# Two of four heads of a recurrent solve written to the other half of the PSUM partitions, with other orders of work in the attentions, a LayerNorm and the first mixer

## The chip, the cores and the metric

The kernel runs on one core of one Trainium2 chip, in one launch. The metric is the time of an execution in device microseconds (us). TensorE (PE) multiplies, VectorE (DVE), ScalarE (ACT) and GpSimd (POOL) do the elementwise work, and SyncE (SP) starts the weight transfers. The engines run their own instruction streams in order and wait for one another through semaphores.

## What is computed

The reference is a chain of small transformer-like blocks over 512 tokens of width 1024, all in float32. Cut to what the change touches:

```python
def _mixer_hgrn2_conv(h, ...):              # "l0"
    proj = h @ w_in                         # q, f, i, g and two halves of a gated unit
    f = lb + (1.0 - lb) * sigmoid(fz)       # the gates; then log(f), its running sum, 1 - f
    o = _hgrn2_chunkwise(silu(qz), f, iz)
    c = _causal_depthwise_conv(glu_a * sigmoid(glu_b), dw_w, dw_b)   # 31 taps
# attentions: xa0 and xa1 (4 heads), moba (8), diff (4 x 2), fox (8), each softmax(q k + bias) v
def _rwkv7_scan(r, w, k, v, kk, a):         # 8 heads of 64
    def step(state, inp):
        sa = einsum('bhij,bhj->bhi', state, -kk_t)
        state = state * w_t + sa * (kk_t * a_t) + v_t * k_t
        return state, einsum('bhij,bhj->bhi', state, r_t)
h = _layer_norm(DEEPNORM_ALPHA * h + ffn, ln2_g, ln2_b)              # "end2"
```

The scan over 512 tokens is done in chunks of 64. In a chunk the tokens' mutual dependence is a triangular system, whose inverse is built by products of 64x64 matrices (squares, fourth and eighth powers of the part inside 16-token blocks, then the part between blocks) and applied to the right sides.

## The kernel before

**Weights.** All weights come from memory as 527 units of 128x1024 floats. SP brings a unit to RW (4 buffers), ACT rounds it to WH (`w_hi`, line 269), POOL subtracts, WL = RW - WH (line 3289), and PE multiplies with it in three passes for each of eight blocks (lines 274 to 276: hi x hi, hi x lo, lo x hi). WH and WL have 3 buffers each (SPLIT = 3), so ACT may round unit u once PE has done unit u - 3. Where in ACT's stream a unit is rounded is written out by hand: each stage calls `w_hi(act, st, v)`, "all units up to v".

**Order.** The program is a list of stages (`PLAN`), `Linear`, `Pairs`, `LayerNorm`, `PairAttention` and free `Stage`s, each of which says what PE, ACT and DVE do in it. An engine walks the list in order. A `st.do(..., name)` marks an instruction, and `st.wait(name)` waits for one.

**l0** (0 to 193 us). Linears for the gated unit, q, f, i and g, with the 31 taps of the convolution spread over DVE and POOL between their outputs; POOL does one tap behind each of a run of units (line 3289 and after). Behind f stand the gates: `h_gates` on DVE (lines 1460 and 1462), then `h_ln`, the logarithm on ACT (line 1468).

**Attention.** `PairAttention` runs over iterations `it`, TT = 4 query blocks for each group of heads, with two streams s. PE: `scores(it)`, then `turn(it - 2)`, which transposes the probabilities of two iterations before; with each fourth turn the `outputs` of a group. ACT: `exps(it)` (line 1212), then the copies `pt` of turned blocks (line 1202). DVE: maxima (1225), `normalize` (1237 to 1247) and `take` (1254). `values` marks an attention whose value products are made in the middle of it.

**LayerNorm.** PE sums (mean, line 1013), ACT squares (1036), PE sums the squares (1003), ACT takes the root (1038), and both write the normalised tensor. Only the norm end2 has `late`, the norm of the next block, that follows at once. The sums into SD that PE waits for are DVE adds (line 691).

**The solve** (1874 to 1996.5 us). The 8 heads are two groups g of four, and there are four blocks t of 128 tokens, two chunks each; a pass is one (t, g), with 9 solve steps (`solve_pe`, `solve_act`, `solve_dve`) and 6 steps of the state. A matrix tensor of a group (D, DT, K, O, F, E) is 128x256: chunk 0 of the four heads in partitions 0 to 63, chunk 1 in 64 to 127, a head in 64 columns. The list `ORDER` lets the second group run 7 steps behind the first (LAG = 7, STEPS = 15), so steps of two passes alternate on every engine. The products of a group go through `quarters` (matmuls on line 2249), which reads a 64x64 block of one partition half and writes the same half of PSUM:

```python
for n in heads:
    for r in halves:
        last = mm(out[r, n * w:(n + 1) * w], L[r, n * 64:(n + 1) * 64], R[r, n, :], start=True, stop=True)
```

Step 1 makes D squared (d2) and its transpose (d2t); step 2 d4, d4t and F2 = F + E F; step 3 d8 and F4; step 4 F8; step 5 the coupling of blocks m, mt, and b0 = F RHS; steps 6 and 7 the corrections b1 and b2. Between them ACT copies the powers from PSUM and DVE adds each F and each right side. Group g uses the PSUM banks from B = 4 g.

## Time and profile before

| | us |
|---|---|
| median of 3 runs | 3428.56 |
| lowest, highest | 3426.52, 3431.85 |
| profiled execution | 3425.99 |
| its span, first to last instruction | 3423.9 |
| PE busy in it | 3297.7 (96%) |
| DVE, ACT, POOL busy | 1337.0, 1204.4, 1329.8 |
| mean granted clock of PE, share of full | 0.989 |

Busy time is the union of an engine's instructions, POOL's included. Idle time of PE is where a released wait can pay. A wait in a list is put down to the instruction that came last before it ended. A timeline row gives the start, the length and the count of like instructions in a row; a group's length runs from its first start to its last end, and a matmul record carries a tail of some 0.22 to 0.28 us beyond the spacing at which such matmuls start. In the windows, PEclk is the granted clock of PE as a share of 2.4 GHz; 0.5 is its lower level, 1.2 GHz.

### The profile page before, as it was taken

How to read it: one execution, taken by the hardware profiler on the slowest of the kernel's cores; microseconds unless marked ns; L12 is line 12 of the kernel's file. 1: busy time of each engine (PE TensorE's matmuls, PEld its weight loads, DVE VectorE, ACT ScalarE, POOL GpSimd, SP SyncE). 2: the span in 40 equal slices, each digit the busy share in tenths (PEclk: the TensorE clock that was granted, in tenths of full speed). 3: DMA queues.
4: the chain of work that ended last, by engine and by line, in shares of the span. 5: the costliest groups of instructions: out<-in, count | busy, mean ns of one | idle time of the engine just before them, and what ended most of it. 6: DMA issues, size and time to landing. Idle time of an engine off the chain costs nothing. (4 is left out here: it accounts for less than half of the span.)

```text
span 3423.9 us, 41030 instructions
## 1 busy us (share of the span) xinstructions
PE 3297.7 (96%) x17376; PEld 2650.1 (77%) x17376; DVE 1337.0 (39%) x1994; ACT 1204.4 (35%) x1817; POOL 1329.8 (39%) x555
## 2 busy tenths in 40 slices
PE   8889999999999999999999999999899999999998
PEld 6678788887778788886677976888688778778886
DVE  8963431214343421213448652001373261134733
ACT  4443432224343422224444333222334432242332
POOL 4743244444254244443143023444344324414442
PEclk9999999999999999999999999999999999999999
DMA  4232132222232122323123032222232212202231
GB/s 154 84 100 87 54 99 98 93 99 92 68 100 98 56 92 99 99 95 104 55 82 125 8 112 75 98 99 97 76 111 93 74 56 99 90 34 99 93 122 68
DMA packets 83005, 302.48 MB, mean 88 GB/s; under 512 B 9060, under 2 KB 10888, under 8 KB 81928
## 3 DMA queue, kind: packets, MB, share of 16 engines
q1 hardware_dynamic: 78368, 280.55, 24.7%
q10 hardware_dynamic: 4456, 19.33, 1.5%
q8 instruction: 137, 2.24, 0.3%
q14 instruction: 44, 0.36, 0.0%
HBM read 290.39 MB, written 9.44 MB: 88 GB/s over the span
## 5 line engine op out<-in xcount | busy, mean ns | idle before, releaser
L3289 POOL TENSOR_TENSOR WL<-RW,WH 128x1024 fp32r<-128x1024 f32 x527 | 1294.1, 2459 | 2067.2 <-ACT WH L269 2066.7
L274 PE MATMUL PS<-XH,WH 128*128 128x512 f32 x2968 | 1169.5, 394 | 46.4 <-DVE XL L932 16.2
L275 PE MATMUL PS<-XL,WH 128*128 128x512 f32 x2968 | 1159.9, 391 | 0.0
L276 PE MATMUL PS<-XH,WL 128*128 128x512 f32 x2968 | 1159.4, 391 | 0.0
L269 ACT ACTIVATE WH<-RW 128x1024 fp32r<-128x1024 f32 x527 | 553.6, 1053 | 799.4 <-PE PS L276 694.3
L274 PEld LDWEIGHTS PS<-XH,WH 128*128 128x128 f32 x2968 | 560.2, 189 | 185.7 <-POOL WL L3289 30.0
L276 PEld LDWEIGHTS PS<-XH,WL 128*128 128x128 f32 x2968 | 560.0, 189 | 117.9
L275 PEld LDWEIGHTS PS<-XL,WH 128*128 128x128 f32 x2968 | 560.4, 189 | 116.3 <-issue 2.2
L274 PE MATMUL PS<-YH,WH 128*128 128x512 f32 (+1 forms) x928 | 350.4, 378 | 8.0 <-POOL WL L3289 6.6
L275 PE MATMUL PS<-YL,WH 128*128 128x512 f32 (+1 forms) x928 | 349.2, 376 | 0.0
L276 PE MATMUL PS<-YH,WL 128*128 128x512 f32 (+1 forms) x928 | 349.1, 376 | 0.0
L501 DVE TENSOR_TENSOR SG<-PS,NR 128x512 f32<-128x512 f32 x136 | 93.5, 691 | 534.3 <-PE PS L276 533.9
L274 PEld LDWEIGHTS PS<-YH,WH 128*128 128x128 f32 x928 | 176.5, 190 | 42.2 <-POOL WL L3289 7.4
L276 PEld LDWEIGHTS PS<-YH,WL 128*128 128x128 f32 x928 | 176.6, 190 | 31.4
L275 PEld LDWEIGHTS PS<-YL,WH 128*128 128x128 f32 x928 | 176.5, 190 | 31.0
L487 ACT ACTIVATE SG<-SG 128x512 f32<-128x512 f32 x80 | 50.6, 632 | 367.7 <-DVE SG L501 367.6
L640 DVE TENSOR_TENSOR YL<-A,YH 128x512 fp32r<-128x512 f32 x66 | 50.3, 773 | 262.6 <-ACT YH L636 262.6
L408 DVE TENSOR_TENSOR A<-PS,NR 128x512 f32<-128x512 f32 (+1 forms) x84 | 53.3, 638 | 164.6 <-PE PS L276 164.2
L636 ACT ACTIVATE YH<-A 128x512 fp32r<-128x512 f32 x66 | 40.7, 629 | 211.3 <-PE PS L276 211.3
L523 DVE TENSOR_TENSOR A<-SG,PS 128x512 f32<-128x512 f32 x30 | 20.6, 688 | 213.9 <-PE PS L276 202.6
L1225 DVE TENSOR_REDUCE SM<-PS 128x1 f32<-128x256 f32 (+3 forms) x128 | 55.6, 470 | 105.2 <-PE PS L3054 55.0
L429 DVE TENSOR_TENSOR X<-X,PS 128x512 f32<-128x512 f32 x40 | 27.5, 687 | 140.4 <-PE PS L276 140.4
(525 smaller groups left out, 3190.3 us busy)
## 6 DMA issues: line engine op xcount, KB each, us to landing
RW<-in_units SPq DMA_DIRECT2D x527, 512.0 KB, 3.3
spill<-X ACTq DMA_DIRECT2D x2, 2048.0 KB, 7.6
X<-in_xT SPq DMA_DIRECT2D x8, 256.0 KB, 5.8
A<-spill ACTq DMA_DIRECT2D x1, 2048.0 KB, 8.9
X<-spill ACTq DMA_DIRECT2D x4, 512.0 KB, 6.0
X<-spill ACTq DMA_DIRECT2D x1, 2048.0 KB, 7.9
out_T<-X ACTq DMA_DIRECT2D x4, 512.0 KB, 3.0
spill<-X ACTq DMA_DIRECT2D x1, 1536.0 KB, 5.1
```

Source lines behind the costliest of these rows:

```text
L269: nc.scalar.activation(WH[:, u % SPLIT, :], RW[:, u % RAW, :], ACT.Copy).then_inc(split_hi, 1)
L274: mm(out, hi, xh, start=first, stop=False)
L275: mm(out, hi, xl, start=False, stop=False)
L276: return mm(out, lo, xh, start=False, stop=last)
L408: ins = nc.vector.tensor_tensor(self.dst(j), bank(e % 4, self.cols), self.late.r, ALU.mult)
L429: ins = nc.vector.tensor_tensor(x, x, b, ALU.add)
L487: st.do(nc.scalar.activation(SG[:, j, :], SG[:, j, :], self.func), f"pair{e}")
L501: st.do(nc.vector.tensor_tensor(dst, bank((e + q) % 4), self.late.r, ALU.mult), name)
L636: st.do(nc.scalar.activation(YH[:, self.hslot(k), :], T(k), ACT.Copy), f"{self.name}.hi{k}")
L640: st.do(nc.vector.tensor_tensor(YL[:, self.hslot(k), :], T(k), YH[:, self.hslot(k), :].bitcast(F32), ALU.subtract), f"{self.name}.lo{k}")
L1225: st.do(nc.vector.tensor_reduce(SM[:, c:c + 1], bank(2 * (it % 2) + s, self.blocks_of(it) * P), AX.X, ALU.max, negate=True), f"{self.id}.m ...
L3289: nc.gpsimd.tensor_tensor(WL[:, u % SPLIT, :], RW[:, u % RAW, :], WH[:, u % SPLIT, :].bitcast(F32), ALU.subtract).then_inc(split_done, 1)
```

## The change

**Solve.** A new function `crossed` makes ten of a pass's products. Heads 0 and 1 write as before, heads 2 and 3 write to the other partition half, in the next bank, and the four (two heads, two halves) stand next to each other in PE's stream. With two such levels a head is back in its half. So that each operand is in the half where the next product reads it, the operands change: F2 = (I + D2) F is now a product alone, with I + D2 made by a DVE add of the identity (p1), the same for p2, p3, pm and pk, and ACT or DVE only copies the results out. F8 and b2 still go through `quarters`. ACT takes half of the copies of the right sides.

**Attention.** In every fourth iteration ACT does the pt copies ahead of the exps. Where there are `values`, the scores of iterations 2 and 3 both stand ahead of the first turn. With `lam` (diff alone) the outputs of a group stand behind the turn of one iteration later, and DVE's take follows.

**LayerNorm end2.** The two unit roundings ahead of the squares now stand one behind the squares and one behind the root.

**l0.** `eager` and `ahead` round each unit one unit earlier in the gated unit, q, f and g. The gates move from DVE to ACT, ahead of the logarithm. POOL's taps begin one unit earlier.

```diff
-                                w_hi(act, st, u + SPLIT)
+                                w_hi(act, st, u + SPLIT + (j in self.ahead))
...
+                            w_hi(act, st, u + SPLIT + self.eager)
...
-                if self.rms is not None or self.late is not None:
+                if self.rms is not None:
                     w_hi(act, st, st.unit + SPLIT - 2)
...
+                if self.late is not None:
+                    w_hi(act, st, st.unit)
...
+                if self.late is not None:
+                    w_hi(act, st, st.unit)
...
-                    if (0 if not self.values else 2) <= it < self.n:
+                    if it == 2 and self.values:
+                        self.scores(st, 2)
+                        self.scores(st, 3)
+                    elif it < self.n and not (it < 4 and self.values):
                         self.scores(st, it)
...
+                    if self.lam is not None and it % TT == 3 and it > TT:
+                        self.outputs(st, it // TT - 1)
                 self.outputs(st, self.groups - 1)
 
             def turn(self, st, it):
-                if it % TT == 0 and it:
+                if self.lam is None and it % TT == 0 and it:
                     self.outputs(st, it // TT - 1)
...
-                    if self.led <= it < self.n:
+                    sooner = it < self.n and it % TT == TT - 1
+                    if self.led <= it < self.n and not sooner:
                         self.exps(st, it)
...
+                    if sooner:
+                        self.exps(st, it)
...
-                    if it % TT == 2 and it >= TT:
+                    if it % TT == (2 if self.lam is None else 3) and it >= TT:
...
+        glu = Pairs("l0.glu", 4, at(0), ACT.Sigmoid, of=1, ready="n0", late=n0, between=glu_dve, between_act=glu_act, eager=1)
...
-        def h_gates(st):
-            st.settle()
+        Linear("l0.f", dst=at(12), func=ACT.Sigmoid, late=n0, between=lambda st, j: conv(st, 5 if j < 3 else 0), between_act=f_act, ahead=range(4))
+
+        vs(lambda st: conv(st, 3))
+
+        def h_ln(act, st, e):
             for h in range(4):
-                st.do(v.tensor_scalar(T(12 + h), T(12 + h), SM[:, LB + 4 + h:LB + 5 + h], SM[:, LB + h:LB + h + 1], ALU.mult, ALU.add))
-            st.settle()
-            st.do(v.tensor_scalar(W2(32, 4), W2(12, 4), -1.0, 1.0, ALU.mult, ALU.add), "h.f")
-            conv(st, 3)
-        vs(h_gates)
-
-        def h_ln(act, st, e):
-            st.wait_ge(*reached("h.f"))
+                st.do(a_.activation(T(12 + h), T(12 + h), ACT.Identity, bias=SM[:, LB + h:LB + h + 1], scale=SM[:, LB + 4 + h:LB + 5 + h]))
+            st.settle()
+            st.do(a_.activation(W2(32, 4), W2(12, 4), ACT.Identity, bias=cst("one"), scale=-1.0), "h.f")
+            st.settle()
             st.do(a_.activation(W2(12, 4), W2(12, 4), ACT.Ln), "h.ln")
...
+        def crossed(b, at, L, R, w=64):
+
+            for n in (0, 2, 1, 3):
+                for r in range(2):
+                    o = halves[r if n < 2 else 1 - r]
+                    last = mm(PS[o, b + n // 2, at + n % 2 * w:at + (n % 2 + 1) * w], L[halves[r], n * 64:(n + 1) * 64], R[halves[r], n, :],
+                              start=True, stop=True)
+            return last
+
...
-                st.wait(i + ".d2t_", i + ".f1")
-                st.do(quarters(bank(B), D, by_head(E)), i + ".d4")
-                st.do(quarters(bank(B + 1), E, by_head(D)), i + ".d4t")
-                st.wait(i + ".rhs")
-                st.do(quarters(bank(B + 2), E, by_head(F), heads=LOW), i + ".f2.0")
-                st.do(quarters(bank(B + 3), E, by_head(F), heads=HIGH), i + ".f2.1")
+                st.wait(i + ".d2t_")
+                st.do(crossed(B, 0, D, by_head(E)), i + ".d4")
+                st.do(crossed(B, 128, E, by_head(D)), i + ".d4t")
+                st.wait(i + ".rhs", i + ".f1", i + ".p1")
+                st.do(crossed(B + 2, 0, K, by_head(F)), i + ".f2")
             elif step == 3:
                 st.wait(i + ".d4t_")
-                st.do(quarters(bank(B), DT, by_head(K)), i + ".d8")
-                st.wait(i + ".F2.0")
-                st.do(quarters(bank(B + 2), K, by_head(F), heads=LOW), i + ".f4.0")
-                st.wait(i + ".F2.1")
-                st.do(quarters(bank(B + 3), K, by_head(F), heads=HIGH), i + ".f4.1")
+                st.do(crossed(B, 0, DT, by_head(D)), i + ".d8")
+                st.wait(i + ".F2", i + ".p2")
+                st.do(crossed(B + 2, 0, E, by_head(F)), i + ".f4")
             elif step == 4:
-                st.wait(i + ".d8_", i + ".F4.0")
-                st.do(quarters(bank(B + 2), E, by_head(F), heads=LOW), i + ".f8.0")
-                st.wait(i + ".F4.1")
-                st.do(quarters(bank(B + 3), E, by_head(F), heads=HIGH), i + ".f8.1")
+                st.wait(i + ".p3", i + ".F4")
+                st.do(quarters(bank(B), K, by_head(F)), i + ".f8")
             elif step == 5:
-                st.wait(i + ".F8.0")
-                quarters(bank(B), F, by_head(O), heads=LOW)
-                st.wait(i + ".F8.1")
-                st.do(quarters(bank(B), F, by_head(O), heads=HIGH), i + ".m")
-                st.do(quarters(bank(B + 2), O, by_head(F)), i + ".mt")
-                st.do(quarters(bank(B + 3), F, RHS[g], P, LOW), i + ".b0.0")
-                st.do(quarters(bank(B + 1), F, RHS[g], P, HIGH), i + ".b0.1")
+                st.wait(i + ".F8")
+                st.do(crossed(B + 2, 0, F, by_head(O)), i + ".m")
+                st.do(crossed(B + 2, 128, O, by_head(F)), i + ".mt")
+                st.do(crossed(B, 0, F, RHS[g], P), i + ".b0")
             elif step == 6:
                 st.wait(i + ".mt_")
-                st.do(quarters(bank(B), D, by_head(DT)), i + ".m2t")
-                st.wait(i + ".q0.0")
-                st.do(quarters(bank(B + 2), DT, RHS[g], P, LOW), i + ".b1.0")
-                st.wait(i + ".q0.1")
-                st.do(quarters(bank(B + 3), DT, RHS[g], P, HIGH), i + ".b1.1")
+                st.do(crossed(B + 2, 0, D, by_head(DT)), i + ".m2t")
+                st.wait(i + ".pm", i + ".q0.0", i + ".q0.1")
+                st.do(crossed(B, 0, E, RHS[g], P), i + ".b1")
             elif step == 7:
-                st.wait(i + ".m2t_", i + ".q1.0")
-                st.do(quarters(bank(B + 1), K, RHS[g], P, LOW), i + ".b2.0")
+                st.wait(i + ".pk", i + ".q1.0")
+                st.do(quarters(bank(B), K, RHS[g], P, LOW), i + ".b2.0")
                 st.wait(i + ".q1.1")
-                st.do(quarters(bank(B), K, RHS[g], P, HIGH), i + ".b2.1")
+                st.do(quarters(bank(B + 1), K, RHS[g], P, HIGH), i + ".b2.1")
...
+                st.wait(i + ".d4t")
+                st.do(a_.activation(pair(D), PS[:, B:B + 2, 0:P], ACT.Copy), i + ".d4_")
+                st.wait(i + ".f1")
+                st.do(a_.activation(pair(DT), PS[:, B:B + 2, P:2 * P], ACT.Copy), i + ".d4t_")
+                st.wait(i + ".f2")
+                st.do(a_.activation(pair(F), PS[:, B + 2:B + 4, 0:P], ACT.Copy), i + ".F2")
             elif step == 3:
-                st.wait(i + ".d8")
-                st.do(a_.activation(E, half(B), ACT.Copy), i + ".d8_")
+                st.wait(i + ".f4")
+                st.do(a_.activation(pair(F), PS[:, B + 2:B + 4, 0:P], ACT.Copy), i + ".F4")
+            elif step == 4:
+                st.wait(i + ".f8")
+                st.do(a_.activation(F, half(B), ACT.Copy), i + ".F8")
             elif step == 5:
-                st.wait(i + ".m")
-                st.do(a_.activation(D, half(B), ACT.Copy))
                 st.wait(i + ".mt")
-                st.do(a_.activation(DT, half(B + 2), ACT.Copy), i + ".mt_")
+                st.do(a_.activation(pair(D), PS[:, B + 2:B + 4, 0:P], ACT.Copy))
+                st.do(a_.activation(pair(DT), PS[:, B + 2:B + 4, P:2 * P], ACT.Copy), i + ".mt_")
+                st.wait(i + ".b0")
+                st.do(a_.activation(RHS[g][:, 2:4, :], by_head(bank(B + 1))[:, 0:2, :], ACT.Copy), i + ".q0.1")
...
-            elif step in (2, 3, 4):
-                name = "248"[step - 2]
-                for h in range(2):
-                    two = slice(128 * h, 128 * h + 128)
-                    st.wait(f"{i}.f{name}.{h}")
-                    if h == 0:
-                        st.settle()
-                    st.do(v.tensor_tensor(F[:, two], F[:, two], bank(B + 2 + h)[:, two], ALU.add), f"{i}.F{name}.{h}")
+                st.wait(i + ".d2_", i + ".w")
+                st.do(v.tensor_tensor(wqc(K), wqc(E), mask("eye"), ALU.add), i + ".p1")
+            elif step == 2:
+                st.wait(i + ".d4_")
+                st.settle()
+                st.do(v.tensor_tensor(wqc(E), wqc(D), mask("eye"), ALU.add), i + ".p2")
+            elif step == 3:
+                st.wait(i + ".d8")
+                st.do(v.tensor_tensor(wqc(K), two_banks(B), mask("eye"), ALU.add), i + ".p3")
             elif step == 5:
...
+                st.wait(i + ".b0")
+                st.do(v.tensor_copy(RHS[g][:, 0:2, :], by_head(bank(B))[:, 0:2, :]), i + ".q0.0")
+                st.wait(i + ".mt_")
+                st.do(v.tensor_tensor(wqc(E), wqc(DT), mask("eye"), ALU.add), i + ".pm")
+            elif step == 6:
+                st.wait(i + ".m2t")
+                st.do(v.tensor_tensor(wqc(K), two_banks(B + 2), mask("eye"), ALU.add), i + ".pk")
+                st.wait(i + ".b1")
+                st.do(v.tensor_copy(RHS[g][:, 0:2, :], by_head(bank(B))[:, 0:2, :]), i + ".q1.0")
+            elif step == 7:
+                st.wait(i + ".b2.0")
+                st.do(v.tensor_copy(RHS[g][:, 0:2, :], by_head(bank(B))[:, 0:2, :]), i + ".q2.0")
...
-                if U0["l0.q"] + 3 <= u < U0["l0.q"] + 3 + POOL_TAPS:
-                    pool_tap(pool, u - U0["l0.q"] - 2)
+                if U0["l0.q"] + 2 <= u < U0["l0.q"] + 2 + POOL_TAPS:
+                    pool_tap(pool, u - U0["l0.q"] - 1)
```

Where the solve's products stand on PE, in the first pass, steps 4 to 6 (SG is where group 0's tensors lie; `scalar_steps` and `vector_steps` are the semaphores of ACT and DVE). Before:

```order
L2249 MATMUL PS<-SG 64x64 [waits vector_steps,scalar_steps]
L2249 MATMUL PS<-SG 64x64 x3
L2249 MATMUL PS<-SG 64x64 [waits vector_steps]
L2249 MATMUL PS<-SG 64x64 x3
L2249 MATMUL PS<-SG 64x64 [waits vector_steps]
L2249 MATMUL PS<-SG 64x64 x3
L2249 MATMUL PS<-SG 64x64 [waits vector_steps]
L2249 MATMUL PS<-SG 64x64 x11
L2249 MATMUL PS<-SG 64x128 x8
L2249 MATMUL PS<-SG 64x64 [waits scalar_steps]
L2249 MATMUL PS<-SG 64x64 x7
```

and after the change (line 2267 is the matmul of `crossed`, 2259 that of `quarters`):

```order
L2259 MATMUL PS<-SG 64x64 [waits scalar_steps,vector_steps]
L2259 MATMUL PS<-SG 64x64 x7
L2267 MATMUL PS<-SG 64x64 [waits scalar_steps]
L2267 MATMUL PS<-SG 64x64 x15
L2267 MATMUL PS<-SG 64x128 x8
L2267 MATMUL PS<-SG 64x64 [waits scalar_steps]
L2267 MATMUL PS<-SG 64x64 x7
```

The four half products of F8 with a wait each became one call behind one wait, m and mt follow behind one wait, and b0 is one call of eight.

ACT around the gates of l0 (269 rounds a unit, 373 is the sigmoid, 1468 the logarithm). Before:

```order
L269 ACTIVATE WH<-RW 128x1024 [waits unit_done,raw_full1]
L373 ACTIVATE A<-A 128x512 [waits vector_steps]
L269 ACTIVATE WH<-RW 128x1024 [waits unit_done,raw_full2]
L373 ACTIVATE A<-A 128x512 [waits vector_steps]
L1419 ACTIVATE A<-PS,VEC 128x512
L1468 ACT_TABLE_LOAD [waits vector_steps]
L1468 ACTIVATE A<-A 128x2048 [waits scalar_steps]
L269 ACTIVATE WH<-RW 128x1024 [waits raw_full3,unit_done,scalar_steps]
L269 ACTIVATE WH<-RW 128x1024 [waits unit_done,raw_full0]
```

and after (1474 and 1476 are the gates, 1478 the logarithm):

```order
L269 ACTIVATE WH<-RW 128x1024 [waits unit_done,raw_full2]
L373 ACTIVATE A<-A 128x512 [waits vector_steps]
L269 ACTIVATE WH<-RW 128x1024 [waits unit_done,raw_full3]
L373 ACTIVATE A<-A 128x512 [waits vector_steps]
L1432 ACTIVATE A<-PS,VEC 128x512
L1474 ACTIVATE A<-A,SM 128x512 [waits scalar_steps]
L1474 ACTIVATE A<-A,SM 128x512 x3
L1476 ACTIVATE A<-A,CST 128x2048 [waits scalar_steps]
L1478 ACT_TABLE_LOAD
L1478 ACTIVATE A<-A 128x2048 [waits scalar_steps]
L269 ACTIVATE WH<-RW 128x1024 [waits raw_full0,unit_done,scalar_steps]
L269 ACTIVATE WH<-RW 128x1024 [waits unit_done,raw_full1]
```

One more rounding stands ahead of the last sigmoid, and the gates stand ahead of the logarithm and of the next rounding.

ACT in moba, iterations 6 to 8 (1212 are exps, 1202 the pt copies). Before:

```order
L1212 ACTIVATE A,SM<-PS,SM 128x384 [waits vector_steps] x2
L1202 ACTIVATE A<-PS 128x128 [waits tensor_steps]
L1202 ACTIVATE SG<-PS 128x128 [waits tensor_steps]
L1212 ACTIVATE A,SM<-PS,SM 128x512 [waits vector_steps] x2
L1202 ACTIVATE A<-PS 128x2x128 [waits tensor_steps]
L1202 ACTIVATE SG<-PS 128x2x128 [waits tensor_steps]
L1212 ACTIVATE A,SM<-PS,SM 128x128 [waits vector_steps] x2
```

and after (1225 and 1213):

```order
L1225 ACTIVATE A,SM<-PS,SM 128x384 [waits vector_steps] x2
L1213 ACTIVATE A<-PS 128x128 [waits tensor_steps]
L1213 ACTIVATE SG<-PS 128x128 [waits tensor_steps]
L1213 ACTIVATE A<-PS 128x2x128 [waits tensor_steps]
L1213 ACTIVATE SG<-PS 128x2x128 [waits tensor_steps]
L1225 ACTIVATE A,SM<-PS,SM 128x512 [waits vector_steps] x2
L1225 ACTIVATE A,SM<-PS,SM 128x128 [waits vector_steps] x2
```

The two copies of 128x2x128 passed the exps of 128x512, the fourth of a group.

## Rows read from the trace of the kernel before

**Rows 1.** The page's first section: busy us, share of the span, instructions of each engine.

```profile
PE 3297.7 (96%) x17376; PEld 2650.1 (77%) x17376; DVE 1337.0 (39%) x1994; ACT 1204.4 (35%) x1817; POOL 1329.8 (39%) x555
```

**Rows 2.** The waits of PE, whole span: us in all, times, longest us.

```profile
PE PS L274 <- POOL WL L3289: 16.4, 9, 5.5
...
PE PS L1170 <- ACT A L1202: 14.9, 12, 2.1
```

**Rows 3.** Windows: length, busy of PE, PEld, DVE, ACT, POOL, PEclk, DMA share, GB/s.

```profile
0.00:193.00 193.00, 164.83 (x776) 135.84 (x776) 163.16 (x206) 81.21 (x103) 117.67 (x62) 0.97 0.36 124
...
915.00:980.00 65.00, 55.34 (x329) 38.57 (x328) 31.26 (x85) 35.90 (x106) 7.16 (x4) 0.89 0.08 25
...
1874.00:1996.50 122.50, 120.30 (x3173) 107.32 (x3172) 74.39 (x210) 42.38 (x115) 4.88 (x2) 1.00 0.10 32
...
2984.00:3056.00 72.00, 64.26 (x319) 47.89 (x318) 32.16 (x84) 33.56 (x98) 4.77 (x2) 1.00 0.04 15
```

**Rows 4.** The timeline of PE in the solve: start us, us, what, out<-in, xcount, [idle before].

```profile
1902.87 0.28 PE L2273 MATMUL PS<-A 64*64 64x64 f32 x3
...
1903.70 0.61 PE L2286 MATMUL PS<-A 64*64 64x128 f32 x13
...
1905.38 1.15 PE L2249 MATMUL PS<-SG 64*64 64x64 f32 x32
...
1915.47 0.93 PE L2249 MATMUL PS<-SG 64*64 64x128 f32 x14
1916.18 0.27 PE L2273 MATMUL PS<-A 64*64 64x64 f32 x3
```

**Rows 5.** The timeline of ACT and of DVE in the solve, step 1.

```profile
1906.11 0.38 ACT L2354 ACTIVATE SG<-PS 128x256 f32<-128x256 f32 x1 [0.40 <-PE PS L2249]
...
1908.44 0.52 DVE L2415 TENSOR_TENSOR SG<-SG,PS 128x128 f32<-128x128 f32 x2 [0.75 <-PE PS L2249]
```

**Rows 6.** Waits of PE in l0, 0 to 193 us, then the timeline there.

```profile
PE PS L274 <- POOL WL L3289: 15.1, 8, 5.5
...
117.69 3.79 DVE L1460 TENSOR_SCALAR A<-A,SM 128x512 f32<-128x512 f32 x4 [0.80 <-ACT A L373]
...
124.11 1.91 ACT L1468 ACTIVATE A<-A 128x2048 f32<-128x2048 f32 x1
...
126.05 2.95 ACT L269 ACTIVATE WH<-RW 128x1024 fp32r<-128x1024 f32 x3
...
129.59 0.79 PE L274 MATMUL PS<-XH,WH 128*128 128x512 f32 x1 [5.35 <-POOL WL L3289]
...
168.42 0.58 PE L274 MATMUL PS<-YH,WH 128*128 128x256 f32 x1 [5.52 <-POOL WL L3289]
```

**Rows 7.** The timeline of ACT and PE in moba, iterations 7 and 8.

```profile
941.49 0.38 ACT L1202 ACTIVATE A<-PS 128x256 f32<-128x256 f32 x1
...
942.02 0.85 PE L1170 MATMUL PS<-CST,A 128*128 128x128 f32 x6 [1.27 <-ACT A L1202]
```

**Rows 8.** Waits of PE in moba, 915 to 980 us.

```profile
PE PS L1170 <- ACT A L1202: 6.2, 4, 2.1
```

**Rows 9.** Waits of PE in fox, 2984 to 3056 us.

```profile
PE PS L1170 <- ACT A L1202: 6.0, 4, 2.1
```

**Rows 10.** The timeline of PE in diff.

```profile
1654.99 0.70 PE L1909 MATMUL PS<-A 64*128 64x256 f32 x4 [0.68 <-ACT A L1212]
```

**Rows 11.** The timeline of DVE, POOL and PE in end2.

```profile
2453.57 0.69 DVE L691 TENSOR_TENSOR SD<-SD,X 128x512 f32<-128x512 f32 x1
...
2456.08 5.09 POOL L3289 TENSOR_TENSOR WL<-RW,WH 128x1024 fp32r<-128x1024 f32 x2 [7.79 <-ACT WH L269]
2456.29 5.43 DVE L691 TENSOR_TENSOR SD<-SD,X 128x512 f32<-128x512 f32 x2
...
2461.87 2.04 PE L1013 MATMUL PS<-SD,CST 128*128 128x512 f32 x2 [6.34 <-DVE SD L691]
```

**Rows 12.** Windows, columns as in rows 3: behind end2's wait.

```profile
2460.40:2470.60 10.20, 7.22 (x18) 1.95 (x18) 6.20 (x9) 5.84 (x9) 0.77 (x1) 0.50 0.21 77
```

More of the change, by code:

```diff
@@ L1431, in glu_dve @@
             conv(st, 4)
-        glu = Pairs("l0.glu", 4, at(0), ACT.Sigmoid, of=1, ready="n0", late=n0, between=glu_dve, between_act=glu_act)
+        glu = Pairs("l0.glu", 4, at(0), ACT.Sigmoid, of=1, ready="n0", late=n0, between=glu_dve, between_act=glu_act, eager=1)
         def q_act(st, j):
@@ L1449, in q_dve @@
                 conv(st, 6)
-        Linear("l0.q", dst=at(8), func=ACT.Silu, late=n0, between=q_dve, between_act=q_act, between_pe=q_pe)
+        Linear("l0.q", dst=at(8), func=ACT.Silu, late=n0, between=q_dve, between_act=q_act, between_pe=q_pe, ahead=range(4))
         def f_act(st, j):
@@ L1516, in g_dve @@
             conv(st, (5, 3, 2, 4)[j])
-        Linear("l0.g", dst=at(20), func=ACT.Silu, late=n0, between=g_dve, between_act=g_act)
+        Linear("l0.g", dst=at(20), func=ACT.Silu, late=n0, between=g_dve, between_act=g_act, ahead=range(4))
         Stage(tensor=lambda pe, st, e: st.wait_ge(*reached("mem.lo7")))
@@ L2353, in solve_act @@
                 st.wait(i + ".d2")
-                st.do(a_.activation(E, half(B), ACT.Copy))
+                st.do(a_.activation(E, half(B), ACT.Copy), i + ".d2_")
                 st.wait(i + ".d2t")
```

34 lines of the change are left out of this document (12 added, 22 removed).

## The prediction

> **What bounds the kernel now.** I read the page's first section, then the waits of PE, then the windows, then the timelines of five stages. PE is busy for 3297.7 of 3423.9 us [rows 1], so the matmuls set the time, and an edit pays only where PE stands idle or where its own work shrinks. The list of PE's waits gives the places: 16.4 us for POOL's WL (one of them 5.5) and 14.9 us in 12 waits for the copies of line 1202 in the attentions [rows 2]. The windows say how dense PE is: 164.83 of 193 us busy in l0, 55.34 of 65 in moba at a clock of 0.89, but 120.30 of 122.5 in the solve [rows 3]. So in the solve only fewer matmul slots can help; elsewhere waits can.
>
> **The solve: matmul slots.** `quarters` issues a 64-column product of four heads as 8 matmuls, which are 16 records (two per fp32 matmul). Two calls, 32 records, take 1.15 us with the last one's own 0.22, so 0.93 for both, 0.466 a call [rows 4]. The 128-column calls: 14 records in 0.93, less 0.27, is 7 starts of a pair 0.11 apart, so 8 pairs or 0.87 for 16 records; two records start together, one from each diagonal quarter. Line 2286 already uses all four quarters: 13 records in 0.61, less 0.28, is four records every 0.11 [rows 4]. `crossed` puts heads 2 and 3 into the other output half and the next bank, so I take four at a time: 0.233 a call of 64 columns, 0.436 for 128. A pass (t, g) has eight 64-column calls of this kind (d4, d4t, f2, d8, f4, m, mt, m2t) and two of 128 (b0, b1): 8 x 0.233 + 2 x 0.436 = 2.74 us less. Over 8 passes that is 21.9 us, the upper bound. d2, d2t, f8 and b2 stay.
>
> Not all of it arrives. The first starts of line 2273 in two passes, 1902.87 and 1916.18, are 13.31 us apart [rows 4]. In a pass, steps of the two groups of heads alternate, so that one group's ACT and DVE work hides behind the other's matmuls. These covers shrink, and each level still needs a copy: the copy of d2 starts at 1906.11, 0.29 us after that call's last matmul, takes 0.38 and lands 0.06 later (0.73 to 0.76), and DVE needs 0.52 for two adds of 128x128 [rows 5]. I laid the new steps out one after the other with the old durations of what stays: PE then waits 0.06 for p1, 0.22 for d4t's copy, 0.05 for F2, 0.29 for the state copy, 0.27 for F8, 0.10 for mt's copy, 0.32 for pm, 0.31 for pk and q1, and 0.24 in rests of a few hundredths, 1.86 in all. The engine is in order, so behind each of these stands the partner's next step, which waits too. A pass takes 13.31 - 2.74 + 1.86 = 12.43, **7 us less in 8 passes**. The identity adds (p1, p2, p3, pm, pk) take the place of the six F adds and of b1's and b2's adds on DVE, and ACT takes half of the q copies; neither is half busy. Ends: 3 us (each of the eight waits 0.06 longer) to 12 (a third of them covered).
>
> The rows show two row halves writing one bank (line 2249) and four quarters writing two banks with each row half in its own (line 2286), not both at once, which is what `crossed` does. The Trainium skill, TensorEngine Tiling (Array Packing), section Restrictions and Gotchas, speaks against it: different row tiles cannot access the same PSUM bank at the same time. By that rule `crossed` would save nothing. The pairs of line 2249 at 0.11 are this very case and run at the pace of line 2286's fours [rows 4], so the trace disagrees.
>
> **l0: the weight splits.** PE's listed waits for WL in 0 to 193 us are eight, 15.1 in all [rows 6]; counted as matmul starts later than the usual 0.227 us they are ten and 16.5, and I go by these. The two large ones: ACT's WH comes at 126.05 because it stands behind Ln (124.11 to 126.02), which stands behind the gates on DVE (117.69 to 121.48, and 1.23 more for the 2048 columns), and PE starts 5.35 late at 129.59; the same again at 168.42 with 5.52 [rows 6]. The change makes each WH one unit earlier, so the unit of 129.59 is split before the last sigmoid of f and its wait goes, as do five small ones in front of it (0.24 + 0.51 + 0.17 + 1.15 + 0.39 = 2.5). What is late next: the following WH, which now stands behind gates on ACT. Four of 128x512 at some 0.67, one of 128x2048 at 1.91 (Ln's size [rows 6]), the table load 1.28 and Ln 1.91 are 7.8 us from about 118.5, so WH ends near 127.4 and WL (2.4) near 129.0 to 129.8, where PE, 2.5 us ahead of its old time, is free at 126.6: 2.4 us. By the same walk 1.4 remains before the scan's units and 4.8 of the 5.52. 16.5 - 8.6 = 7.9, **8 us less**. Ends: 6 (the gates 1 us longer, and again at the second place) and 9.5 (with the clock, below). The pool taps, a unit earlier, stand where POOL waited for WH, at nothing; were POOL late there, each costs what the unit's WL slips.
>
> **The attentions.** In every fourth iteration ACT's exps (two of 0.69 plus reads) stand ahead of the pt copies, and PE's next turn waits for these: in moba the copy at 941.49, PE at 942.02 after 1.27 idle [rows 7]. Copies first lets that turn start 1.1 us earlier, but exps end 0.7 later and the next scores wait for them, so 0.5 is left, twice. Moba's four waits of this kind are 6.2 in all [rows 8], the first and the last near 2; these have no such successor, and the scores moved ahead help the first: 2.0 + 1.0 + 1.2 = **4.2** (2.5 to 6). Fox has four too, 6.0 in all [rows 9]; by the same working 0.8 + 2 x 0.6 + 1.3 = **3.3** (2 to 4.5). Diff: 0.68 at 1654.99 [rows 10], twice, and a little at its ends, of which the outputs moved behind the turn cover some: **1.6** (0.5 to 2.5). The two cross-attentions: 0, between -0.6 and +0.6, as their copies gain what their exps lose.
>
> **end2.** Two WH at 2454.95 feed two WL (2456.08, 5.09 us for both), beside which two sum adds on DVE take 5.43 together where one alone takes 0.69; PE waits 6.34 for them [rows 11]. With the WH behind the squares and the root: 5.43 - 1.38 = 4.05, and something of the half clock after the wait (0.50 for 10.2 us [rows 12]), 0.5 to 1. Back comes up to 1 where WL meets line 932, which also reads two tensors of SBUF. **4.5 less** (3 to 5.5). What hides the moved splits: PE does not need them before 2477. The Trainium skill, GPSIMD Engine Reference, section Key points, says that GpSimd shares its SBUF interfaces with VectorE and contends with instructions of two SBUF inputs; by that rule the steps of 2464 to 2476 that read PSUM lose nothing, and the trace agrees for the adds of line 691, which read two and are the slow ones [rows 11].
>
> **Sum.** 7 + 8 + 4.2 + 3.3 + 1.6 + 4.5 = 28.6. The profiled execution took 3425.99 (span 3423.9), so 3397.4; the median of the runs lies 2.57 above it: **3400**. All terms at their good ends give 12 + 9.5 + 6 + 4.5 + 2.5 + 5.5 + 0.6 = 40.6, or 3388; at their poor ends 3 + 6 + 2.5 + 2 + 0.5 + 3 - 0.6 = 16.4, or 3412.
>
> **Rivals.**
> *A, PE stays the bound in the solve.* For it: the stage has hardly a wait now [rows 3]. Against: turnarounds of 0.75 us [rows 5] beside covers of 0.23 to 0.47. It gives 15 more: 3385.
> *B, the waits come back in the in-order ACT queue.* The later exps, gates and copies make half of the gains of l0 and the attentions vanish (8.5), and the solve gives 4: 3400 + 8.5 + 3 = 3411. For it: a wait of 1.27 is worth 0.5 in my own working. Against: the first and last turns, and end2, have nothing behind.
> *C, crossing quarters do not overlap.* Then `crossed` costs what `quarters` did, the solve gains nothing and pays 1.86 x 8 = 15 of waits where its new chains are longer: 3400 + 7 + 15 = 3422. Against: rows 4, as above.
> *D, slower: the clock.* After end2's wait the granted clock was 0.50 (1.2 GHz, half of 2.4) for 10.2 us [rows 12], and in moba, where PE was busy 85% and no wait of rows 8 passes 2.1, its mean was 0.89 [rows 3]. The solve's PE share falls from 98% to 85%. At half clock its 8 x 10.57 = 85 us of matmuls need 85 more, with the 15 of waits covered: +70, 3470. It decides against the change from 41% of the stage (28.6 / 70). Against: fox, with waits as long and PE busy 89%, kept 1.00 [rows 3, 9].
>
> **Chances.** Forecast 0.58, A 0.13, B 0.19, C 0.05, D 0.05. The range 3388 to 3412 takes in the forecast with its bounds and B. A measurement of this kernel tells some 0.2% (7 us) from no change: faster is forecast, A and B, 0.90; within it C, 0.05; slower D, 0.05.
>
> **What would show it.** In the solve, groups of four records per 0.057 us in `crossed` and passes 12.4 us apart (A: 10.6; C: 13.3 or more; D: clock 0.5). In l0, no wait at the unit after f and a wait of 2 to 3 us one unit later. In moba and fox, the turn's wait under 0.3 and a new one of scores for ACT exps. In end2, the sum adds at 0.69 and PE's wait near 2.3. I am wrong if the solve's turnarounds are longer or better covered than laid out, or if the gates on ACT take well over 4.6 us.

## The result, and the profile after

The changed kernel takes 3394.6 us (median of 4 runs, 3392.35 to 3397.95) against 3430.2 us for the kernel before in the same comparison: a ratio of 0.9898, with a 95% interval of 0.9881 to 0.9915, so 29 to 41 us less. The ratio and its interval are worked out from all runs of both kernels, so they need not be the quotient of two medians, here or below. The forecast was 3400, its range 3388 to 3412, and it had 28.6 us less. The profiled execution took 3397.95 (span 3396.1), 27.8 us less in the span than the profiled one before.

In the lines below an engine's idle time ahead of an instruction stands in square brackets, with what ended it. The page of the kernel after, first section, answers to [rows 1]:

```profile
PE 3285.8 (97%) x17376; PEld 2633.8 (78%) x17376; DVE 1320.4 (39%) x1957; ACT 1218.5 (36%) x1854; POOL 1330.2 (39%) x555
```

PE is busy 11.9 us less, the rest of the 27.8 is idle time that went. The waits of PE over the whole span, in all, times, longest, answer to [rows 2]:

```profile
PE PS L274 <- POOL WL L3311: 4.9, 4, 2.2
...
PE PS L1014 <- DVE SD L692: 2.3, 1, 2.3
PE PS L1818 <- ACT A L1225: 2.3, 3, 1.5
...
PE PS L3071 <- ACT X L1225: 2.2, 3, 1.5
...
PE PS L1180 <- ACT A L1213: 1.4, 4, 0.3
```

The 16.4 us for POOL's WL are 4.9. The 14.9 us in 12 waits for the pt copies are 1.4 in 4; new in their place are waits of scores for exps (lines 1818 and 3071), 2.3 and 2.2 us. The windows, with the columns of rows 3, are of l0, moba, diff, the solve and fox:

```profile
0.00:182.00 182.00, 162.14 (x776) 135.06 (x776) 154.36 (x201) 86.88 (x107) 118.54 (x62) 0.99 0.38 131
...
904.00:965.00 61.00, 54.98 (x366) 39.32 (x365) 35.56 (x88) 38.27 (x110) 11.68 (x6) 1.00 0.11 35
1613.00:1669.00 56.00, 51.62 (x240) 33.89 (x239) 32.87 (x77) 28.16 (x83) 4.88 (x2) 0.91 0.06 21
1857.90:1973.30 115.40, 108.74 (x3173) 90.96 (x3172) 70.03 (x177) 51.40 (x147) 4.86 (x2) 1.00 0.11 34
...
2958.00:3028.00 70.00, 65.53 (x321) 48.33 (x321) 33.09 (x87) 34.88 (x105) 5.43 (x3) 1.00 0.05 16
```

The same weight multiplications stand in the same order in both traces, so the start of one and the same matmul can be compared ahead of a stage and behind it. That gives what each stage gained, in us, for two traces of the changed kernel (the second is experiment e7), beside the forecast:

| stage | forecast | first trace | second trace |
|---|---|---|---|
| l0 | 8 | 11.2 | 11.2 |
| moba | 4.2 | 8.5 | 7.8 |
| diff | 1.6 | -1.7 | 0.1 |
| solve | 7 | 7.1 | 6.2 |
| end2 | 4.5 | 3.6 | 4.6 |
| fox | 3.3 | 2.7 | 2.6 |
| everything else | 0 | -4.3 | -2.0 |
| sum to the last weight multiplication | 28.6 | 27.1 | 30.5 |

**The solve.** The timeline of PE in the solve answers to [rows 4]:

```profile
1885.76 0.27 PE L2294 MATMUL PS<-A 64*64 64x64 f32 x2
...
1888.36 1.15 PE L2259 MATMUL PS<-SG 64*64 64x64 f32 x32
...
1890.00 1.13 PE L2267 MATMUL PS<-SG 64*64 64x64 f32 x48
...
1891.48 0.73 PE L2267 MATMUL PS<-SG 64*64 64x64 f32 x32
...
1897.96 0.27 PE L2294 MATMUL PS<-A 64*64 64x64 f32 x2
```

Line 2267 is `crossed`. The 48 records of d4, d4t and f2 take 1.13 us, less the last one's 0.22 and a gap of 0.19 between two starts ahead of f2, which waits for p1: 0.72, or 0.24 a call, where a `quarters` call is still 0.466 (32 records of line 2259 in 1.15). d8 and f4 are 32 records in 0.73 less 0.22, 0.255 a call. The marks of two passes, 1885.76 and 1897.96, are 12.20 apart; the seven marks of the stage give 15.25, 12.54, 12.20, 12.35, 12.38, 12.35 and 12.29, where the trace before has 15.23, 13.40, four times 13.31, and 13.44.

**l0.** The timeline of ACT, then of POOL, around the gates answers to [rows 6]:

```profile
110.81 1.06 ACT L269 ACTIVATE WH<-RW 128x1024 fp32r<-128x1024 f32 x1 [1.06 <-PE PS L276]
113.64 0.63 ACT L373 ACTIVATE A<-A 128x512 f32<-128x512 f32 x1 [1.77 <-DVE A L408]
...
114.88 2.94 ACT L1474 ACTIVATE A<-A,SM 128x512 f32<-128x512 f32 x4
117.85 2.01 ACT L1476 ACTIVATE A<-A,CST 128x2048 f32<-128x2048 f32 x1
...
121.18 1.92 ACT L1478 ACTIVATE A<-A 128x2048 f32<-128x2048 f32 x1
123.12 2.01 ACT L269 ACTIVATE WH<-RW 128x1024 fp32r<-128x1024 f32 x2
...
112.39 2.41 POOL L3311 TENSOR_TENSOR WL<-RW,WH 128x1024 fp32r<-128x1024 f32 x1
...
124.26 2.40 POOL L3311 TENSOR_TENSOR WL<-RW,WH 128x1024 fp32r<-128x1024 f32 x1 [6.57 <-ACT WH L269]
```

The unit that came 5.35 us late is rounded at 110.81, ahead of the last sigmoid of f at 113.64. The next unit's WL ends at 126.66, and PE starts it without a wait: in 60 to 137 us the list of PE's waits is empty.

**end2.** The timeline answers to [rows 11]:

```profile
2433.84 1.42 DVE L692 TENSOR_TENSOR SD<-SD,X 128x512 f32<-128x512 f32 x2
...
2435.40 2.04 PE L1014 MATMUL PS<-SD,CST 128*128 128x512 f32 x2 [2.32 <-DVE SD L692]
...
2444.11 2.34 POOL L3311 TENSOR_TENSOR WL<-RW,WH 128x1024 fp32r<-128x1024 f32 x1 [18.27 <-ACT WH L269]
...
2447.13 2.06 DVE L1087 SCALAR_TENSOR_TENSOR X<-A,VEC,PS 128x512 f32<-128x512 f32 x3 [0.74 <-PE PS L1025]
2447.20 2.36 POOL L3311 TENSOR_TENSOR WL<-RW,WH 128x1024 fp32r<-128x1024 f32 x1 [0.74 <-ACT WH L269]
...
2449.42 0.75 DVE L933 SCALAR_TENSOR_TENSOR XL<-X,VEC,XH 128x512 fp32r<-128x512 f32 x1 [0.23 <-ACT XH L923]
```

The last two adds of line 692 take 1.42 us together instead of 5.43, and PE waits 2.32 instead of 6.34. The two WL stand at 2444.11 and 2447.20, and line 933 takes its usual 0.75; it meets the second for its last 0.14 us only.

**moba.** The timeline of ACT and PE answers to [rows 7]:

```profile
925.48 0.38 ACT L1213 ACTIVATE A<-PS 128x256 f32<-128x256 f32 x1 [1.34 <-PE PS L1180]
...
926.03 0.69 ACT L1225 ACTIVATE A<-PS,SM 128x512 f32<-128x512 f32 x1
...
926.29 0.84 PE L1180 MATMUL PS<-CST,A 128*128 128x128 f32 x6
...
927.53 0.30 PEld L1818 LDWEIGHTS PS<-A 64*128 64x128 f32 x4 [0.63 <-ACT A L1225]
```

The copy stands ahead of the exps of the fourth iteration, PE's turn follows at 926.29 without a wait, and the scores at 927.53 wait 0.39 for the exps.

### The profile page after: what moved, and what is told of

It is laid out like the page before. It is cut to its first block and busy times, and to the rows that moved or that the text cites. A ratio compares the mean times of both kernels' runs of the same rounds, so it can differ in the third digit from the quotient of the medians.

```text
span 3396.1 us, 41017 instructions
## 1 busy us (share of the span) xinstructions
PE 3285.8 (97%) x17376; PEld 2633.8 (78%) x17376; DVE 1320.4 (39%) x1957; ACT 1218.5 (36%) x1854; POOL 1330.2 (39%) x555
```

## The experiments

All times are medians; the kernel before has 3429.43 in the first comparison, 3430.34 in the second and 3430.07 in the third. Stage gains are read as above.

**One part at a time.** Each kernel is the one before with one part of the change, whole: the solve (e1), `PairAttention` (e2), l0 (e3), the LayerNorm (e4). One line of each, in this order:

```diff
-                st.do(quarters(bank(B), D, by_head(E)), i + ".d4")
+                st.do(crossed(B, 0, D, by_head(E)), i + ".d4")
...
-                    if self.led <= it < self.n:
+                    if self.led <= it < self.n and not sooner:
...
-                                w_hi(act, st, u + SPLIT)
+                                w_hi(act, st, u + SPLIT + (j in self.ahead))
...
-                if self.rms is not None or self.late is not None:
+                if self.rms is not None:
```

> The kernel before with the solve part alone (crossed, its copies and identity adds). The two traces put the solve stage 7.1 us shorter. Theory 1 (turnarounds fill the covers, passes 12.4 us apart): 7 us less, about 3423 against 3430, ratio 0.998. Theory 2 (the solve alone gives the matmul slots in full, the rest was lost elsewhere): 22 us less, ratio 0.994. Theory 3 (half-clock windows decide the total): the stage is 7 us shorter in the trace, and the total is anywhere within 4 us of that.

> The kernel before with the orders of PairAttention alone. Theory 1 (waits of PE released, by the trace of after: moba 5.9, fox 3.1, diff 1.9, cross-attentions 0): 11 us less, ratio 0.9968. Theory 2 (as forecast, 9 us). Theory 3 (the 8.5 us of moba between the traces hold 2.6 us of half clock that come and go): the stall sums stay, the stage times of moba and diff move by up to 3.4 us with the windows of half clock.

> The kernel before with the l0 part alone (earlier splits, gates on ACT, taps a unit earlier). Theory 1 (waits 16.5 to 8.0 and less half clock): 8.5 to 11 us less, ratio 0.997. Theory 2 (part of the 11 us between the traces was a chance of the start): about 6 us less. The unit after f starts without a wait; the waits of 1.2, 1.0, 2.3, 2.2 and 1.2 us in the scan's part stay.

> The kernel before with the two splits of end2 moved, alone. Theory 1: the adds of line 691 take 0.7 us each, PE waits 2.3 instead of 6.3, 4 us less, ratio 0.9988. Theory 2 (the shared traffic of POOL and DVE is not the cause, the adds wait for something else): no change. The windows of half clock behind it decide another -1 to +1 us.

| kernel | median | ratio, 95% interval | gain of its own stages by the trace |
|---|---|---|---|
| e1, solve | 3419.79 | 0.9978 (0.9969 to 0.9986) | solve 7.8 |
| e2, attention | 3416.36 | 0.9967 (0.9954 to 0.9979) | moba 8.5, fox 2.6, diff 0.0 |
| e3, l0 | 3420.64 | 0.9965 (0.9951 to 0.9978) | l0 11.2 |
| e4, norm | 3425.60 | 0.9988 (0.9979 to 0.9996) | end2 4.5 |

The ratios are 0.22, 0.33, 0.35 and 0.12% less, 1.02% in all, and the whole change is 1.02% less: the parts add up. They do so within their intervals, which are some 0.1% either way for each part. Each theory 1 holds, for the attentions by the traces, as the total can't tell 11 us from 9. e1 gives 7.5 us (4.8 to 10.6), not the 22 of the matmul slots alone. In e4 the adds of line 691, with the splits out of the way:

```profile
2458.63 1.42 DVE L691 TENSOR_TENSOR SD<-SD,X 128x512 f32<-128x512 f32 x2
...
2460.19 1.10 PE L1013 MATMUL PS<-SD,CST 128*128 128x512 f32 x2 [2.32 <-DVE SD L691]
```

**All but the solve.** e5 is the changed kernel with the solve as before.

```diff
-                st.do(crossed(B, 0, D, by_head(E)), i + ".d4")
+                st.do(quarters(bank(B), D, by_head(E)), i + ".d4")
...
```

> The changed kernel with the solve as before (attention, norm and l0 changed). If the parts add up, it lies 7 us above the changed kernel: about 3402, ratio 0.992 against before. If the solve works through later windows of the clock, the distance is 3 to 11 us.

It took 3399.98, 0.9911 (0.9896 to 0.9925) of before, 5.2 us above the changed kernel of the same comparison. By the trace its solve stage is 0.5 us shorter than before, the changed kernel's 6.2 to 7.1. With intervals of 0.15% for each kernel the distance does not speak against 7, nor does it say more.

**The order of the four heads.** e6 calls neighbours that use the same quarter.

```diff
-            for n in (0, 2, 1, 3):
+            for n in (0, 1, 2, 3):
```

> The changed kernel with the heads of crossed in the order 0, 1, 2, 3 instead of 0, 2, 1, 3, so that two neighbours use the same quarter. Theory 1 (an in-order engine, a matmul waits only for its own quarter): a call takes 3 slots instead of 2, 0.35 instead of 0.24 us for 64 columns, unless the next call follows at once and takes the free quarters; 10 calls and 8 passes, of which about half stand alone: 4 to 9 us more than the changed kernel. Theory 2 (the four quarters overlap only by luck of the queue, order does not matter): no change. Theory 3 (crossing matmuls are serial with the others when not neighbours): 20 us more.

3396.62 against 3394.81, ratio to before 0.9903 (0.9888 to 0.9918), and by the trace a solve gain of 6.1 against the control's 6.2. Theory 2 is nearest: the order makes no measurable difference. The timeline of PE in e6:

```profile
1888.33 1.13 PE L2267 MATMUL PS<-SG 64*64 64x64 f32 x47
...
1889.83 0.76 PE L2267 MATMUL PS<-SG 64*64 64x64 f32 x32
```

47 records in 1.13 us and 32 in 0.76, as with the other order. So two neighbours in the same quarter do not hold up those behind them by a measurable time; in which way they are taken up is not shown. What both orders share is that the heads are spread over all four quarters. The variant with all four products in one bank, where two row halves would write the same bank and the same 64 partitions, wasn't tried, and no run shows what it would do.

**The control.** e7 is the changed kernel again.

> The changed kernel unaltered, as a control on this chip and for a second trace. If the windows of half clock belong to the program, they lie where they lay (243.9, 1541, 1622.9, 1841.3, 2059.8, 2070, 2435.3, 2448.9, 2684.4). If they depend on how an execution falls against a clock of its own, some of them move or change length, and stage times differ by 1.7 to 5 us at the same waits.

3394.81 (ratio 0.9898, 0.9883 to 0.9912), the same as the first comparison. Its span is 3392.7, 3.4 us less than the first trace, with the same program. The first trace's windows of moba (904 to 965 us) and diff (1613 to 1669) stand above; here is its window of 1838 to 1852 us, then all three of e7:

```profile
1838.00:1852.00 14.00, 10.95 (x46) 9.21 (x45) 13.65 (x17) 8.52 (x12) 5.53 (x3) 0.76 0.23 76
```

```profile
904.00:965.00 61.00, 56.74 (x361) 40.45 (x360) 35.20 (x86) 38.00 (x109) 10.93 (x6) 0.94 0.11 35
1613.00:1669.00 56.00, 51.64 (x248) 34.33 (x247) 32.76 (x77) 29.39 (x85) 4.87 (x2) 0.94 0.08 26
1838.00:1852.00 14.00, 10.95 (x50) 9.65 (x50) 13.65 (x17) 9.12 (x13) 4.87 (x2) 0.88 0.23 76
```

The granted clock is 1.00 and 0.94 in moba, 0.91 and 0.94 in diff, 0.76 and 0.88 just ahead of the solve. PE's waits in diff and ahead of the solve are the same in both: what differs is the clock. (In moba e7 has 1.5 us less of waits of scores for exps, 0.8 against 2.3, and a lower clock in return.) That settles the two stages that the table had on the wrong side. In diff the first trace lost 1.7 us and the second gained 0.1; ahead of the solve the first lost 2.7 and the second 1.6, in a stage that the change doesn't touch, and e1 to e4 lost 1.3 to 1.6 there as well. The trace before has full clock in that place. In diff the clock hides what the order of the work gains, as the next experiment shows.

**diff without its own move.** e8 is the changed kernel with `outputs` and `take` of diff where they were.

```diff
-                    if self.lam is not None and it % TT == 3 and it > TT:
-                        self.outputs(st, it // TT - 1)
...
-                if self.lam is None and it % TT == 0 and it:
+                if it % TT == 0 and it:
...
-                    if it % TT == (2 if self.lam is None else 3) and it >= TT:
+                    if it % TT == 2 and it >= TT:
```

> The changed kernel without the move of outputs and take in diff (those with lam). Theory 1 (diff's waits fell from 7.0 to 5.1 by the exps behind the copies as well as by the outputs): 0.3 to 1 us more than the changed kernel. Theory 2 (the move keeps the ring of banks busier and costs): up to 1 us less.

3395.14 (0.9897, 0.9881 to 0.9914): no difference from 3394.81. By the trace diff is 0.3 us shorter than before, in the control 0.1. So neither theory can be read from the time. The waits of scores for exps and the window of diff can be read, of the control first:

```profile
PE PS L1919 <- ACT A L1225: 1.9, 2, 1.5
```

```profile
PE PS L1917 <- ACT A L1223: 3.2, 4, 1.5
...
1613.00:1669.00 56.00, 50.40 (x249) 33.71 (x248) 32.72 (x77) 29.70 (x85) 4.87 (x2) 0.97 0.08 27
```

Without the move these waits are 1.3 us longer, and PE is busy 50.40 us of the 56 against 51.64. It is the same in all traces: 1.9 us in 2 waits in the seven with the move, 2.9 to 3.2 in the seven without. So the move does release 1.3 us, somewhat more than theory 1 has. The granted clock takes it back: it is 0.94 in the control, 0.97 in e8. At a like clock the gain shows: e1 and e4, with diff as before and 0.94, lost 1.3 us in the stage, while the control with 0.94 gained 0.1.

**Only ACT's order in the attentions.** e9 is the kernel before with one edit.

```diff
-                    if self.led <= it < self.n:
+                    sooner = it < self.n and it % TT == TT - 1
+                    if self.led <= it < self.n and not sooner:
                         self.exps(st, it)
...
+                    if sooner:
+                        self.exps(st, it)
```

> The kernel before with one edit of the attentions alone: ACT's pt copies ahead of the exps in every fourth iteration. In the trace with all orders a period of moba fell from 11.06 to 10.10 us, which my working put at 0.5. Theory 1 (the copies alone do that, the early scores only help the start): period 10.1, fox's period 13.5 instead of 14.05, cross-attentions within 0.3, total 9 to 11 us less. Theory 2 (the early scores set all later iterations ahead too): period 10.6, total 5 to 7 us less.

3419.14, ratio 0.9969 (0.9958 to 0.9981), 11 us less, all that e2 gives. Moba gained 8.55 (e2 8.52), fox 2.67 (e2 2.63), diff 0.2. The period of moba is 10.09. Theory 1 holds: the early scores added nothing, and diff's outputs nothing to the time (their 1.3 us of released waits went into the clock, as above). PE's waits in moba in e9:

```profile
PE PS L1170 <- DVE A L1245: 1.5, 1, 1.5
PE PS L1811 <- ACT A L1215: 1.2, 3, 0.5
PE PS L1184 <- ACT SG L1203: 0.8, 1, 0.8
PE PS L1170 <- ACT A L1203: 0.3, 1, 0.3
```

The 6.2 us for the copies [rows 8] are 0.3.

**The splits of l0 without the gates.** e10 is the kernel before with the earlier splits and taps, the gates left on DVE.

```diff
-                                w_hi(act, st, u + SPLIT)
+                                w_hi(act, st, u + SPLIT + (j in self.ahead))
...
-                            w_hi(act, st, u + SPLIT)
+                            w_hi(act, st, u + SPLIT + self.eager)
...
-                if U0["l0.q"] + 3 <= u < U0["l0.q"] + 3 + POOL_TAPS:
-                    pool_tap(pool, u - U0["l0.q"] - 2)
+                if U0["l0.q"] + 2 <= u < U0["l0.q"] + 2 + POOL_TAPS:
+                    pool_tap(pool, u - U0["l0.q"] - 1)
```

> The kernel before with l0's earlier splits and taps, but the gates left on DVE. With the gates on ACT l0 got 11.1 us shorter. Theory 1 (the splits do it, the gates only follow): 10 to 11 us here too, with no wait at the unit after f. Theory 2 (the gates on DVE hold ACT's logarithm, and it the next split, until about 122.7): a wait of 1 to 3 us one unit later, l0 8 to 9 us shorter. Theory 3 (without the gates DVE is late for its taps): the waits in the scan's part are longer than with the gates on ACT.

3416.85, ratio 0.9965 (0.9953 to 0.9978), not to be told from e3. By the trace l0 is 9.8 us shorter, with the gates on ACT 11.2. There is no wait at the unit after f. The logarithm runs on ACT at the same time either way:

```profile
114.34 0.67 ACT L1420 ACTIVATE A<-PS,VEC 128x512 f32<-128x512 f32 x1
...
121.00 1.92 ACT L1469 ACTIVATE A<-A 128x2048 f32<-128x2048 f32 x1
122.95 2.01 ACT L269 ACTIVATE WH<-RW 128x1024 fp32r<-128x1024 f32 x2
```

at 121.00 in e10, 121.18 with the gates on ACT. So the splits are what gained; theory 2's wait does not come. The 1.4 us between 9.8 and 11.2 are not in the waits: the list of PE's waits from 60 to 190 us adds up to 8.7 us in e10 and 8.5 in e3, and the mean clock is 0.98 and 0.99. Of theory 3 there is this much, waits that changed places: PE's waits for DVE (line 408) are 5.6 us in e10 and 2.9 in e3, those for POOL 0.7 and 3.2:

```profile
PE PS L274 <- DVE A L408: 5.6, 2, 3.6
...
PE PS L274 <- POOL WL L3290: 0.7, 1, 0.7
```

```profile
PE PS L274 <- POOL WL L3287: 3.2, 2, 2.2
PE PS L274 <- DVE A L408: 2.9, 2, 2.0
```

**The lag of the two groups.** e11 and e12 are the changed kernel with the second group 8 or 6 steps behind.

```diff
-        LAG = 7
+        LAG = 8        # e12: 6
```

> The changed kernel with the second group of the solve 8 steps behind instead of 7, so that other steps lie between a product and the next that needs it. A pass has 1.9 us of waits now, at the turnarounds. If their covers are what counts, the pass changes from 12.35 to between 12.0 and 12.9 us, the stage by up to 4 us either way; if the in-order queues of ACT and DVE set them, it stays within 0.1.

> As the run with 8 steps, with 6: the pass at 12.0 to 12.9 us if the covers count, 12.35 if the queues of ACT and DVE do. One of the two should be the better one if 7 was tuned for the longer matmuls of before.

3396.79 with 8 (0.9906, 0.9892 to 0.9919) and 3396.83 with 6 (0.9901, 0.9888 to 0.9915), neither to be told from the changed kernel, and neither beats it. The traces tell more. The marks of the passes are some 10.9 and 14.2 to 14.6 apart in turn with 8 and with 6: two passes take 25.05 to 25.4 us, with 7 they take 24.6 to 25.0. The covers count, then, as the first case of e11 has it. For the whole stage that decides only against 8, which is 3.8 us shorter than before, against 6.2 and 7.1 with 7. With 6 it is 6.7 us shorter: the first pass ends sooner (the first two marks are 13.75 apart, with 7 they are 15.25), and that pays for the longer passes. Between 6 and 7 nothing is decided.

## Why the prediction was right

**The bound and the sum.** The time lay in the range and the forecast was the likeliest case. The sum was 28.6 and the comparison gives 35.6 (29 to 41). The parts add up, so each term can be looked at by itself. The total alone would not tell the forecast from rival A: 3394.6 lies between 3400 and A's 3385. The experiments tell them apart, as the extra came from l0 and moba and not from the solve.

**The solve (7 forecast, 6.1 to 7.8 in five traces).** The price of a call (0.233) measured 0.24 to 0.26, a pass 12.20 to 12.54 where 12.43 was laid out, and the new waits are of the size and mostly in the places named. The long gaps between starts of matmuls in the pass from 1885.76, with a usual 0.06 still in them, are 0.19 ahead of f2 (p1, forecast 0.06 of waiting), 0.26 ahead of the state step (0.29), 0.23 ahead of m (F8, 0.27), 0.30 ahead of b1 (pm, 0.32) and 0.40 ahead of b2 (pk and q1, 0.31). Two that the working had, 0.22 at d4t's copy and 0.10 at mt's copy, are not among them. The 0.40 ahead of d2 stands in the trace before too, as 0.38. Rival A (22 us) fell with e1, rival C with the records of `crossed`, which start four to a 0.06 us slot. The rule of the Trainium skill that was weighed there (TensorEngine Tiling (Array Packing), Restrictions and Gotchas: no two row tiles in one PSUM bank at once) does not hold as it stands: `crossed` keeps four quarters writing two banks, and each bank is written by both row halves at once, into different partition halves, at 0.24 us a call. Both row halves in the same partition half of one bank, no run shows.

**l0 (8 forecast, 11.2 measured).** PE's late starts fell from 16.5 to 8.0 us (1.2, 1.0, 2.3, 2.2 and 1.2), the working had 8.6, so the sum of the waits was right and the places were not. The step that failed is "about 118.5": the gates began at 114.88, since the last sigmoid of f, and all of ACT's work before it, came earlier together with PE. I had moved PE ahead and left ACT where it was. So the 2.4 us wait behind f never came, and others remained. The waits gave 8.5 us. The other 2.7 are the clock, which the term left out: its mean was 0.97 over 193 us before [rows 3] and is 0.99 over 182 us after.

**Attention (9.1 forecast; 11.1 to 11.4 in e2 and e9).** Fox was 3.3 and is 2.6 to 2.7. Moba was 4.2 and is 7.8 to 8.5. Two steps failed, and the clock was left out. "Exps end 0.7 later" in the working of the period: ACT had been idle for 1.7 us ahead of these exps, waiting for the maxima, and the copies fit into that time. With respect to PE's turn ahead of them (939.34 before, 925.04 after) the exps start 0.81 us behind it before and 0.99 after: 0.18 later, not 0.7. So a period gained 0.97 (11.06 to 10.09), not 0.5. The timeline of the kernel before, PE and ACT ahead of [rows 7]:

```profile
939.34 0.62 PE L1170 MATMUL PS<-CST,A 128*128 128x128 f32 x4
...
940.15 0.69 ACT L1212 ACTIVATE A<-PS,SM 128x512 f32<-128x512 f32 x1 [1.71 <-DVE SM L1225]
```

The 1.71 in brackets is the idle time into which the copies went. And the clock again: its mean was 0.89 over 65 us before [rows 3] and is 1.00 or 0.94 after. How much of moba's extra is clock can be told from e1, which leaves moba alone: it gained 1.2 us there, at a mean clock of 0.95 over 914 to 979 us. The second trace, with 0.94, gained 7.8. So the waits are worth about 6.6 us (an estimate from these two traces), and not 4.2. The two periods make 1.0 of the difference; how the rest divides among the first and the last turns is open. "With the scores moved ahead, 2.0" failed on the other side: the early scores gained nothing (e9), as the wait only moved from the turn to the maxima's DVE work and the exps (1.7 and 1.5 us at the start of moba in the trace after). In diff the 1.6 does not arrive: the stage gained 0.0 to 0.3 in e2, e7, e8 and e9 and lost 1.7 in the first trace. 1.3 us of waits did go, all by the outputs behind the turn, to which the working gave only some of the term; the copies ahead of the exps released none, as in e9, with that order alone, PE waits 2.9 us for the exps in diff as before. What failed is that released waits were taken for time at an unchanged clock: it was lower with the outputs moved (0.91 or 0.94 in six traces, 0.97 in e11) than without (0.97 in five, 0.94 in e1 and e4).

**end2 (4.5 forecast, 4.6 in the second trace, 4.5 in e4).** The wait fell from 6.34 to 2.32, as worked out. The up to 1 us that was to come back at line 933 did not: it took 0.75, but it begins only 0.14 us before the WL ends (2447.20 to 2449.56), so it is no test. The rule of the Trainium skill (GPSIMD Engine Reference, Key points) agrees with the traces for the adds of line 691, 0.71 us each without a WL beside them and 2.7 with one. It agrees for steps that read PSUM too: the three of line 1087 take 2.06 us beside a WL, and 2.06 in the trace before (line 1082), with none beside them.

**Rivals B and D.** B (the waits come back in ACT's queue) is seen in small: 4.5 us of waits of scores for exps are new. But it was not half of the gain. D did not come: the clock in the solve is 1.00 throughout, with PE busy 94% by the window. The 85% that I had put there is 10.57 of 12.43, worked out from starts of matmuls, and is no measure to set beside the 98% of a window.

**The total.** The profiled execution before was a quick one: 3425.99, where the medians of three later comparisons are 3429.4 to 3430.3. I added 2.57 for that, the comparison had 4.2. The execution of the second trace after is 31.4 us shorter than that one (3394.55); with the 4.2 this makes the 35.6 of the medians. Against the 28.6 of the sum, l0 and moba have 6.8 more in it. By the estimates above some 2.9 of that are waits (0.5 and 2.4) and some 3.9 the clock. Diff, the solve and fox have 3.0 less, end2 0.1 more, and 2.0 are lost outside the stages. That errors of both signs cancel to within 6 us of the forecast is in part luck.

## What to carry to other kernels

When PE does 64x64 blocks, count quarters before counting instructions: here a product of four blocks costs half as much once its heads are spread over all four quarters, and then the copies between dependent products are the bound, so the gain was a third of what the slots promised. Before moving an instruction ahead of another on an in-order engine, look at whether that engine was idle there: a copy that fits into a wait costs the one behind it nothing. And when a stage gets earlier, move all its engines in the working, not only the one that waited. A stage's time holds both waits and clock: read the two apart, in every kernel with an edit and without it, before calling the edit worth nothing.

## What was not expected of the hardware

The granted clock falls to its lower level in other places, and for other lengths, from one execution to the next of the same program: 0.91 and 0.94 over the same 56 us of diff, 1.00 and 0.94 over moba, 0.76 and 0.88 over 14 us ahead of the solve, and a stage whose code and waits are the same gains or loses 1.3 to 3.1 us by it. In e3, which does not touch fox, fox took 3.1 us more than before, at a mean clock of 0.95 over 69 us (before 1.00 [rows 3]):

```profile
2979.00:3048.00 69.00, 61.27 (x292) 45.35 (x291) 31.93 (x82) 31.31 (x94) 2.36 (x1) 0.95 0.03 8
```

A difference of one stage between two single traces below some 3 us says nothing, unless the waits themselves differ.
